# Modulation products in four column strips, and the first banded attention in batches of four heads

## The reference

```python
qb = q.reshape(B, nb, WINDOW, SWA_KV_HEADS, SWA_GROUP, HEAD_DIM)
kb, vb = band(k), band(v)               # the block before and the block itself
s = jnp.einsum('bnqhgd,bnkhd->bnhgqk', qb, kb) * (HEAD_DIM ** -0.5) + bias
s = jnp.where(mask, s, NEG_INF)
p = jax.nn.softmax(jnp.concatenate([s, sink], axis=-1), axis=-1)[..., :-1]
o = jnp.einsum('bnhgqk,bnkhd->bnqhgd', p, vb)
```

```python
mod = jax.nn.silu(c) @ w_ada + b_ada        # c: one row of 1024
mod_c = jax.nn.silu(c_ctx) @ w_ada + b_ada
```

## Time and profile before

| | |
|---|---|
| median of 3 runs | 2503.81 us (2503.61 to 2506.11) |
| span of the profiled execution | 2500.4 us |
| PE busy | 2411.0 us (96%) |
| DVE busy | 1599.2 us (64%) |
| ACT busy | 1248.2 us (50%) |
| POOL busy | 751.4 us (30%) |
| modulation and bias turn on PE | 54.38 to 85.95 us |
| banded attention on PE | 269.51 to 358.31 us |

### The profile page before, as it was taken

One profiled execution on the slowest core, in us unless ns is written; L12 is line 12 of the kernel. 1 busy time (PEld: TensorE's weight loads), 2 busy tenths in 40 slices (PEclk: granted clock), 3 DMA queues, 4 the chain that ended last, 5 costly groups with the idle time before them and its releaser, 6 DMA issues.

```text
span 2500.4 us, 32413 instructions
## 1 busy us (share of the span) xinstructions
PE 2411.0 (96%) x11302; PEld 1886.2 (75%) x11302; DVE 1599.2 (64%) x2478; ACT 1248.2 (50%) x1874; POOL 751.4 (30%) x396
## 2 busy tenths in 40 slices
PE   8999899999999999999999999999997999999996
PEld 6587567778788878878788778766764878878885
DVE  4033887756563357675442734687247999999998
ACT  4111555434543432443333411377245888888887
POOL 0312100114444477334466331120311132123310
PEclk9999999999999999999999999999998999999998
DMA  6210000022222264222233211000438999999996
GB/s 241 98 49 3 35 1 1 1 101 87 91 93 101 95 241 151 84 85 91 93 118 112 73 61 40 34 1 1 153 141 309 402 395 388 380 391 385 392 390 234
DMA packets 86602, 384.08 MB, mean 154 GB/s; under 512 B 7980, under 2 KB 9180, under 8 KB 71520
## 3 DMA queue, kind: packets, MB, share of 16 engines
q1 hardware_dynamic: 81744, 365.25, 38.7%
q0 software_dynamic: 4752, 17.43, 2.6%
HBM read 361.60 MB, written 21.05 MB: 153 GB/s over the span
## 4 chain that ended last, share of the span: by engine, by line
PE 49%; issue 11%; DVE 7%; POOL 4%; ACT 2%; DMA 1%; SPq 0%; POOLq 0%; DVEq 0%; ACTq 0%
PE ps L997 10%; PE ps L999 9%; PE ps L998 9%; PE ps L1367 5%; PE ps L1369 5%; PE ps L1368 5%; POOL w_lo L2816 4%; DVE e_lo L2672 3%; PE ps L1202 2%; PE ps L1192 1%; DMA arena<-in_w_gate 1%; PE ps L1274 1%; PE ps L1403 1%; DMA residual_rows<-arena 0%; PE ps L1181 0%
## 5 line engine op out<-in xcount | busy, mean ns | idle before, releaser
L2816 POOL TENSOR_TENSOR w_lo<-arena,w_hi 128x1024 fp32r<-128x1024 f32 x188 | 457.5, 2434 | 702.4 <-ACT w_hi L1608 700.1
L2672 DVE TENSOR_TENSOR e_lo<-arena,e_hi 128x1024 fp32r<-128x1024 f32 x384 | 451.3, 1219 | 35.4 <-ACT e_hi L1940 30.6
L1940 ACT ACTIVATE e_hi<-arena 128x1024 fp32r<-128x1024 f32 x384 | 401.3, 1059 | 88.1 <-PE ps L1369 82.0
L1608 ACT ACTIVATE w_hi<-arena 128x1024 fp32r<-128x1024 f32 x188 | 198.4, 1055 | 367.0 <-PE ps L999 366.9
L997 PE MATMUL ps<-h_hi,w_hi 128*128 128x512 f32 x848 | 336.4, 397 | 8.4 <-POOL w_lo L2816 5.3
L999 PE MATMUL ps<-h_hi,w_lo 128*128 128x512 f32 x848 | 332.0, 391 | 0.0
L998 PE MATMUL ps<-h_lo,w_hi 128*128 128x512 f32 x848 | 331.7, 391 | 0.0
L1367 PE MATMUL ps<-e_hi,x_hi 128*128 128x512 f32 x512 | 205.0, 400 | 7.2 <-DVE e_lo L2672 4.4
L1369 PE MATMUL ps<-e_lo,x_hi 128*128 128x512 f32 x512 | 200.2, 391 | 0.0
L1368 PE MATMUL ps<-e_hi,x_lo 128*128 128x512 f32 x512 | 200.0, 391 | 0.0
L997 PEld LDWEIGHTS ps<-h_hi,w_hi 128*128 128x128 f32 x848 | 160.4, 189 | 48.5 <-issue 12.2
(11 more groups left out here) (388 smaller groups left out, 5091.2 us busy)
## 6 DMA issues: line engine op xcount, KB each, us to landing
arena<-in_w_up SPq DMA_DIRECT2D x108, 1024.0 KB, 8.0
arena<-in_w_down SPq DMA_DIRECT2D x86, 1024.0 KB, 7.7
arena<-in_w_gate SPq DMA_DIRECT2D x64, 1024.0 KB, 10.0
arena<-in_w_in SPq DMA_DIRECT2D x18, 1024.0 KB, 4.8
arena<-in_w_out SPq DMA_DIRECT2D x16, 1024.0 KB, 4.8
arena<-in_w_ada SPq DMA_DIRECT2D x12, 1024.0 KB, 13.7
arena<-in_w_ada SPq DMA_DIRECT2D x24, 512.0 KB, 6.7
routed_rows<-arena SPq DMA_DIRECT2D x8, 520.0 KB, 7.5
```

The costliest lines, as they stand in the source:

```text
L1608: act_e.activation(w_hi[:, q, :], slot[c][:, q * D:(q + 1) * D], ACT.Copy).then_inc(s_whi, 1)
L1940: act_e.activation(e_hi[:, (2 * sl + a) % RING, :], slot[sl][:, a * D:(a + 1) * D], ACT.Copy).then_inc(s_ehi, 1)
L2672: v.tensor_tensor(e_lo[:, r, :], slot[sl][:, a * D:(a + 1) * D], e_hi[:, r, :].bitcast(F32), ALU.subtract).then_inc(s_elo, 1)
L2816: gp.tensor_tensor(w_lo[:, q, :], slot[c][:, q * D:(q + 1) * D], w_hi[:, q, :].bitcast(F32), ALU.subtract).then_inc(s_wlo, 1)
```

## The change

The modulation weights are used in two quads, (0, 1, 3, 4) and (7, 2, 6, 5). In a quad the product of each k goes to its own 32 partitions of the output (`ps[32 * j:32 * j + 32, ...]`), with a stationary operand of 32 columns, of which two are meant; so the four partial sums stand in four strips of the same bank. rowA takes all 128 rows, and `columns` multiplies with a constant ("pick") that adds the strips. The weights' buffers and the order of their loads change; item 0 of w_in is loaded before the last weights; ACT splits its two tiles as soon as the first quad is used; POOL's second constant waits for the end of the modulation, and w_out's loads wait for the end of the banded attention.

The banded attention goes by 16 quads of four heads (b; block n = b // 2). DVE still takes the maxima head by head. The sink stands as one more column before the scores (sw_raw has 257), so one exponential takes both and their sum. The transposes of a quad fill banks 4 (near block) and 5 (far block), which ACT and DVE copy with 512 columns each; eight value products follow, then one reciprocal of four columns and one product of 256 columns. The loops are written out.

```diff
-        rowA = view(156, 2 * D)[0:2]
+        rowA = view(156, 2 * D)
...
-            for k in range(4):
+            def modulation_weights(k):
                 sp.dma_start(adaA[k], ada[k, :, 0:2 * D]).then_inc(s_al[k], 16)
+            for k in (0, 1, 3, 4):
+                modulation_weights(k)
             sp.wait_ge(s_bld, 16)
             sp.wait_ge(s_h, 2)
             sp.wait_ge(s_sq, 2)
             sp.dma_start(mflip, bass.AP(ext_d, 0, [[1, P], [384, 8], [1, 256]])).then_inc(s_bias, 16)
-            for k in (4, 7):
-                sp.dma_start(adaA[k], ada[k, :, 0:2 * D]).then_inc(s_al[k], 16)
-            sp.wait_ge(s_au, 1)
-            sp.dma_start(adaA[5], ada[5, :, 0:2 * D]).then_inc(s_al[5], 16)
+            modulation_weights(7)
+            sp.wait_ge(s_h, 4)
+            sp.wait_ge(s_sq, 4)
+            modulation_weights(2)
+            sp.dma_start(slot[0], T["w_in"][:, 0:ITEM]).then_inc(wl[0], 16)
             sp.wait_ge(s_bc, 1)
-            sp.dma_start(adaA[6], ada[6, :, 0:2 * D]).then_inc(s_al[6], 16)
-
-
-            for i in range(7):
-                if i < 2:
-                    sp.wait_ge(s_au, 5)
+            modulation_weights(6)
+            sp.wait_ge(tps, 2 * T_IN)
+            modulation_weights(5)
+            for i in range(1, 7):
+                if i == 1:
...
+            sp.wait_ge(s_pv, U_DENSE)
...
-            def modulation(k, w, load, b, n):
-
-                pe.wait_ge(*load)
-                for c in range(n):
-                    m = pe.matmul(ps[0:2, b + c, :], scT[:, k, :], w[:, c * 512:(c + 1) * 512], start=(k == 0), stop=(k == KT - 1))
-                return m
-
             def columns(row, n, rows):
                 pe.wait_ge(s_row, rows)
                 for t in range(n):
-                    m = pe.transpose(ps[:, 4, 2 * t:2 * t + 2], row[:, t * P:(t + 1) * P], ident[0:2, 0:2])
+                    m = pe.matmul(ps[:, 4, 2 * t:2 * t + 2], row[:, t * P:(t + 1) * P], con("pick"), start=True, stop=True)
                 m.then_inc(s_mod, 1)
-            def modulations(ks):
-
-                for i in ks:
-                    k = ADA_ORDER[i]
-                    modulation(k, adaA[k], (s_al[k], 16), 4, 4).then_inc(s_au if k < KT - 1 else s_ad, 1)
+            def modulations(quad):
+                for k in ADA_QUADS[quad]:
+                    pe.wait_ge(s_al[k], 16)
+                for c in range(4):
+                    for j, k in enumerate(ADA_QUADS[quad]):
+                        m = pe.matmul(ps[32 * j:32 * j + 32, 4 + c, :], sc_wide[:, 2 * k:2 * k + 32], adaA[k][:, c * 512:(c + 1) * 512], start=(quad == 0), stop=(quad == 1))
+                m.then_inc(s_ad if quad else s_au, 1)
...
-            modulations(range(2))
+            modulations(0)
             pe.wait_ge(s_bias, 16)
             bias_turned(range(2, 4))
-            modulations(range(2, 4))
             pe.wait_ge(evv, 4)
             pe.wait_ge(eva, 4)
             bias_turned(range(2)).then_inc(s_flip, 1)
-            modulations(range(4, KT))
+            modulations(1)
...
+            def swa_scores(b, cs):
+                n, g, w = b // 2, b % 2, sw_keys(b)
+                if cs[0] == 0:
+                    pe.wait_ge(s_stage, n + 1)
+                if b >= 2:
+                    pe.wait_ge(s_max, 4 * (b - 2) + cs[-1] + 1)
+                for c in cs:
+                    m = pe.matmul(sw_scores(b, c), qs[n % 2][:, 4 * g + c, :], swak[:, (n + 1) * P - w:(n + 1) * P], start=True, stop=True)
+                    if c % 2:
+                        m.then_inc(s_S, 2)
+            def swa_turned(b, cs):
+                if cs[0] == 0 and b:
+                    pe.wait_ge(s_pt, 4 * b)
+                for c in cs:
+                    pe.wait_ge(s_exp, 4 * b + c + 1)
+                    for j in range(sw_keys(b) // P):
+                        m = pe.transpose(ps[:, 4 + j, c * P:(c + 1) * P], sw_probs[b % 2][:, c, 1 + j * P:1 + (j + 1) * P], ident)
+                if cs[-1] == 3:
+                    m.then_inc(s_T, 4)
+            def swa_values(b):
+                n, g, nb = b // 2, b % 2, sw_keys(b) // P
+                pe.wait_ge(s_pt, 4 * b + 4)
+                if b >= 2:
+                    pe.wait_ge(s_o, 4 * (b - 1))
+                for c in range(4):
+                    for j in range(nb):
+                        m = pe.matmul(ps[:, 6 + b % 2, c * HD:(c + 1) * HD], sw_turned[b % 2][j][:, c * P:(c + 1) * P], swav[:, n + 1 - nb + j, g * HD:(g + 1) * HD],
+                                      start=(j == 0), stop=(j == nb - 1))
+                m.then_inc(s_pv, 4)
...
-            units(U_SWA, swa(0, 0))
-            units(8, swa(1, 1), swa(0, 0))
-            with pe.Fori(1, NT // 2) as m:
-                for b in range(2):
-                    units(m * 16 + 8 * b, swa(2 * m + b, b), swa(2 * m + (b - 1), 1 - b))
+            swa_scores(0, range(4))
+            swa_scores(1, range(4))
+            for b in range(2 * NT):
+                for cs in (range(2), range(2, 4)):
+                    swa_turned(b, cs)
+                    if b + 2 < 2 * NT:
+                        swa_scores(b + 2, cs)
+                if b < 2 * NT - 1:
+                    swa_values(b)
...
+            act_e.wait_ge(s_au, 1)
+            for n in range(2):
+                first_high(n)
             act_e.wait_ge(s_flip, 2)
             act_e.activation(swab.rearrange("p a b -> p (a b)"), banks(0, 2048), ACT.Copy).then_inc(s_n1, 1)
-            for n in range(2):
-                first_high(n)
...
+            def swa_exp(b, c):
+                i, w = 4 * (b % 2) + c, sw_keys(b) + 1
+                act_e.wait_ge(s_max, 4 * b + c + 1)
+                if b >= 2 and c == 0:
+                    act_e.wait_ge(s_T, 4 * (b - 1))
+                    act_e.wait_ge(s_o, 4 * (b - 1))
+                act_e.activation(sw_probs[b % 2][:, c, 0:w], sw_raw[b % 2][:, c, 0:w], ACT.Exp, bias=sw_nmax[:, i:i + 1], scale=-1.0,
+                                 accum_out=sw_den[:, i:i + 1]).then_inc(s_exp, 1)
+            def swa_near_out(b):
+                act_e.wait_ge(s_T, 4 * b + 4)
+                if b >= 2:
+                    act_e.wait_ge(s_pv, 4 * (b - 1))
+                act_e.activation(sw_turned[b % 2][0], ps[:, 4, :], ACT.Copy).then_inc(s_pt, 2 if b >= 2 else 4)
+            act_e.wait_ge(s_ssi, 2)
+            for b in range(2 * NT):
+                swa_exp(b, 0)
+                if b:
+                    swa_near_out(b - 1)
+                for c in range(1, 4):
+                    swa_exp(b, c)
+                if b % 2 and b > 1:
+                    group_square(0, b // 2 - 1, 8 * (b // 2))
+            swa_near_out(2 * NT - 1)
...
+            def swa_max(b, c):
+                i, h, w = 4 * (b % 2) + c, 4 * (b % 2) + c, sw_keys(b)
+                v.wait_ge(s_S, 4 * b + c // 2 * 2 + 2)
+                if b >= 2:
+                    v.wait_ge(s_exp, 4 * (b - 2) + c + 1)
+                v.tensor_tensor_reduce(sw_raw[b % 2][:, c, 1:1 + w], sw_scores(b, c), swab[:, h, 256 - w:256], -1.0, sinkB[:, 0, h:h + 1],
+                                       ALU.add, ALU.min, sw_nmax[:, i:i + 1]).then_inc(s_max, 1)
+            def swa_far_out(b):
+                v.wait_ge(s_T, 4 * b + 4)
+                if b >= 4:
+                    v.wait_ge(s_pv, 4 * (b - 1))
+                v.tensor_copy(sw_turned[b % 2][1], ps[:, 5, :]).then_inc(s_pt, 2)
+            def swa_out(b):
+                n, four = b // 2, slice(4 * (b % 2), 4 * (b % 2) + 4)
+                v.wait_ge(s_pv, 4 * b + 4)
+                vc_.link(v.reciprocal(sw_rec[:, four], sw_den[:, four]))
+                v.tensor_tensor(mixed[:, n, b % 2 * 256:b % 2 * 256 + 256].rearrange("p (a b) -> p a b", a=4), ps[:, 6 + b % 2, 0:256].rearrange("p (a b) -> p a b", a=4),
+                                sw_rec[:, four].unsqueeze(2).to_broadcast([P, 4, HD]), ALU.mult).then_inc(s_o, 4)
...
+            for c in range(4):
+                swa_max(0, c)
+            for b in range(2 * NT):
+                if b + 1 < 2 * NT:
+                    for c in range(2):
+                        swa_max(b + 1, c)
+                if b:
+                    swa_out(b - 1)
+                if b + 1 < 2 * NT:
+                    for c in range(2, 4):
+                        swa_max(b + 1, c)
+                if b >= 2:
+                    swa_far_out(b)
```

More of the change, by code:

```diff
@@ L50 @@
 _at = 0
-for _n, _w in (("ident", P), ("causal", P), ("left", P), ("mean", P), ("swap16", P), ("swap32", P), ("flip", P), ("slot", 1)):
+for _n, _w in (("ident", P), ("causal", P), ("left", P), ("mean", P), ("swap16", P), ("swap32", P), ("flip", P), ("slot", 1), ("pick", 2)):
     CONST[_n] = (_at, _w)
@@ L478, in pair_columns @@
             return ps[:, 7, :]
-        def value_bank(w, dense):
-            return 6 if dense else 6 + w % 2
         def score_bank(u):
@@ L983, in late_turned @@
                     i.then_inc(s_flip, 1)
```

(9 more changed lines are left out.)

94 lines of the change are left out of this document (32 added, 62 removed).

## The result

| | before | after |
|---|---|---|
| median | 2503.71 us (2499.09 to 2506.11, 4 runs) | 2468.78 us (2467.59 to 2470.87, 4 runs) |
| ratio of the times | | 0.9865, 95% interval 0.9851 to 0.9879 |
| span of the profiled execution | 2500.4 | 2469.1 |
| modulation starts on PE | 54.38 | 56.72 |
| from there to tile 0 | 31.57 | 10.78 |

The forecast was 2471.0; the kernel takes 2468.8, by the ratio 1.35% less than before. The spans of the two profiled executions differ by 31.3 us, where the forecast's sum was 32.8; the medians differ by 34.9, because the profiled execution after is the slowest of its four, and the one before was faster than its median. The ledger of the two spans is the difference of the table's rows: start +2.3, modulation -20.8, tile 0 to scores +6.6, attention -19.1, rest -0.3, in all -31.3.

A forecast was written before the change was run, and what follows sets the result against it. PE was taken to bound the modulation, and DVE, with PE close behind, the banded attention. Forecast: 2500.4 - 13.9 (strips) + 2.6 (sums) - 21.5 (batches) = 2467.6, plus 3.4 around the span, 2471.0 us; range 2461 to 2487.

The forecast's parts named there:

- The strips: Modulation on PE: products in four strips half overlap, eight groups taking 13.9 us instead of 27.8, gain 13.9.
- Rival 1: Modulation: the four strips overlap fully, another 6.9 us off, 2464.1 us in all; chance 0.27.
- half overlap: Modulation: program order lets strip 1 start only beside strip 0's second record; 1.74 us a group, chance 0.42.
- full overlap: Modulation: all four strips run together, a group costing what one product does; gain 20.8 us, chance 0.27.
- The sums: PE, adding the strips: 32 matmul records replace 16 transposes, 3.7 us against 1.14, cost 2.6.
- Tile 0: First projection tile: split weights and bias copy ready 5 us ahead, or 1.6 with full overlap; no cost.
- The batches: Banded attention in quads of four heads: PE becomes the bound, gain 21.5 us; bounds 25 and 12.5.
- The cycle: Banded attention, steady part: one quad takes 4.5 us, bounds 4.2 and 5.2, for 13 cycles.
- The fill: Banded attention, first scores until the transposes of quad 2: about 6.8 us.
- Rival 3: Banded attention: copy before the value products exposed each time, 0.7 us a quad, 10 lost, 2481 us; chance 0.14.
- Rival 2: Modulation: strips do not overlap and gain nothing, summing costs 2.6, 2484.9 us in all; chance 0.13.
- Rival 4: Banded attention: TensorE's clock falls, some 65 us more if throughout, 2503 to 2537 us in all; chance 0.04.

The follow-up runs named there:

- one_strip: Kernel after, with all modulation products sent to strip 0 and the sums reading only those 32 rows: 2497.52 us, one run.
- strip_by_strip: Kernel after, with a quad's two loops exchanged so that four products of one strip stand in a row: 2475.81 us, one run.
- both_edits: Kernel after, with sums four at a time behind tiles 0 to 3 and each attention quad's scores after all its transposes: 2465.07 us, ratio 0.9850.
- sums_apart: Kernel after, with all 16 sums moved one tile ahead of the mean, behind tile 3: 2466.25 us, one run.
- transposes_thrice: Kernel before, with its sixteen 2-row transposes done three times over: 2507.1 us, one run.
- both_again: both_edits run once more, on one chip with the unaltered kernel after: 2465.24 us, ratio 0.9841.
- scores_last: Kernel after, with all transposes of an attention quad first and then all its scores: 2469.66 us, ratio 0.9874.
- strips_only: Kernel before, with only the strips, their sums and the moved loads: 2487.44 us, ratio 0.9936.
- batch_only: Kernel before, with only the batched attention and w_out's loads behind it: 2490.55 us, ratio 0.9940.
- sums_spread: Kernel after, with the 16 sums placed four each behind projection tiles 1 to 4: 2467.21 us, ratio 0.9857.

## Why the prediction was right, step by step

- **The strips** (gain 13.9 forecast, 20.8 measured): the step that failed is the supposition that PE starts its records in program order and that a second record of strip 0 holds back strip 1. Rival 1 held, to a tenth of a us: 8 groups take 7.2 us without the bias turn. one_strip and strip_by_strip show it: the records wait for their own strip, and a few that wait are passed. I had given half overlap 0.42 and full overlap 0.27. The two records of a product were a correct reading; what I drew from them about the start was not in any row.
- **The sums** (+2.6 forecast, +2.4 measured, 3.49 against 1.08): right, 0.109 a record against 0.115. (The row quoted for the 0.115, 1.95 us for 16, gives 0.122; the sum would have been 2.8.)
- **Tile 0** waits for nothing: right, and by the times of the full-overlap case: high parts until 62.4, low parts until 66.3, second quad done at 67.5. The cover forecast at 1.6 us is 1.2.
- **The batches** (gain 21.5 forecast, 19.1 measured; dense scores 69.7 us behind the first banded ones, 66.3 forecast). The cycle was right in its kind and nearly in size: 4.56 on the mean (267.22 to 326.44 in 13 cycles) against 4.5, PE the bound, DVE idle, the copy exposed by 0.13 where 0.05 was forecast. In it the transposes were over-counted (0.89 for 1.1) and the values under-counted: 1.84 for 1.55, 16 records at 0.115. The 0.39 of the earlier trace rows was the distance to the scores behind a unit's four value records; in a row of sixteen PEld is busy throughout (1.86), one load every 0.11 us, and the first load waits for the copy. The fill was 9.6 for 6.8: transposes of quad 2 stand behind the scores of quads 2 and 3, two times 1.75 us of PE, which the sum left out. With 2.8 us against 0.7 for the 13 cycles it is the larger miss of the two. Timeline of PE, the fill:

```profile
257.64 1.95 PE L938 MATMUL ps<-arena 128*128 128x128 f32 x16
260.57 0.71 PE L949 MATMUL ps<-const,arena 128*128 128x128 f32 x2 [0.98 <-ACT arena L1626]
261.12 1.04 PE L938 MATMUL ps<-arena 128*128 128x256 f32 x4
...
267.22 0.61 PE L949 MATMUL ps<-const,arena 128*128 128x128 f32 x4
```

- **Rival 3** (copy exposed by 0.7 a quad) did not come: 0.13. **Rival 2** did not: 3.6 a quad, not 14.
- **Rival 4** (the clock falls in the attention, and the kernel is slower) did not come: 1.00 from 258 to 326. (Short falls in that stage came in other executions, as in both_edits, and cost 1.7 us there.) But its mechanism came at a place where I had not looked, behind the sums, and smaller: the mean +1.6, shown by sums_apart, transposes_thrice and both_again to hang on how long the row of short records ahead of it is. With the slower tiles around 130 and falls between 225 and 255, tile 0 to the scores grew by 6.6, of which the sums are 2.4. Falls between 220 and 255 stand in eight of the ten executions with the new modulation stage or one_strip's form of it, at changing places (both_again: 0.66 at 245 to 250), but not in scores_last and strip_by_strip, and in none of the three with the old one. I have no cause for them.
- **The start** (+2.3, not forecast). The granted clock was 0.68 in the value products, at 20 to 25, where before it was 1.00:

```profile
20.00:25.00 5.00, 5.00 (x22) 5.00 (x21) 5.00 (x5) 5.00 (x6) 0.00 (x0) 0.68 1.01 423
```

 This start is there in both runs of the kernel after, in strips_only, one_strip, strip_by_strip, scores_last and both_again, and not in the kernel before, batch_only and transposes_thrice; but also not in sums_spread, sums_apart and both_edits, of which the last is the same program as both_again. So it is not tied to the program alone. Nor does the wait for n_lo just ahead of these products explain it: it is 1.57 us in the kernel before and 2.04 to 2.09 in all twelve others, with the fall or without. Of the kernels with the new modulation stage the three without the fall start it at 54.9 to 55.1 and the seven with it at 56.4 to 56.9; so some 1.7 of the 2.3 are the clock, and what tips it stays open.

That the total came so near was luck. In the sum an underrated gain of 6.9 met three costs that were not foreseen: 2.4 in the attention, some 4.2 of clock and tiles between tile 0 and the scores, 2.3 at the start. So the span fell 1.5 us less than the 32.8 forecast. The median came out 2.2 under the forecast all the same, for two reasons. The execution profiled after was 2.1 slower than its median. And the 3.4 us "around the span" mixed two things: 1.8 lies outside the span (2470.87 against 2469.1), and the other 1.6 was the distance of one execution from the median of several. The range, 2461 to 2487, had its lower end from full overlap, so it held what happened and not only the number.

## What to carry to other kernels

Products with few output rows gained nearly fourfold here when four of them went to four column strips, with neighbours in the program in different strips: the order (3.6, 8.9 or 13.9 us a quad here) is as much of the gain as the strips are. When a latency-bound loop is batched, count everything PE issues between the first score and the first steady cycle, and time a row of short matmuls by the pace of such a row (0.11 us a record here, with PEld busy throughout), not by the distance to whatever followed one of them. Do not put short matmuls side by side with other short ones: spread them between full tiles, since the cost (1.6 us on the mean, and tiles behind it) falls on instructions that nobody changed.

## What the runs showed of the hardware

- Two-record float32 products in four column strips overlap fully in alternating order: 32 records of 512 columns take 3.58 us from start to start, where one strip takes 13.85, a factor of 3.9. Four products in a row to the same strip give 8.8.
- TensorE's granted clock fell to its lower level while the profile had PE busy without a gap: behind 3 to 3.5 us of records with 2 columns or in the last of them, and through the records with one column (0.56 and 0.76 in two stretches of 5 us); with 1.1 us of them ahead it came later and shallower (0.70), or not at all. The Trainium skill, in "TensorE: Matmul & The Clock Gate", Part 1: The HAM clock gate, speaks of gaps between matmuls as what lets the clock fall; these rows show a fall with none between the records that the profile draws, whose ends are modelled.
- Executions of one kernel differ, and loosely with the mean granted clock: the kernel before gave spans of 2497.0 at 0.991 and 2505.4 at 0.985, but also 2501.1 and 2506.8 at 0.987. The two traces of one program, both_edits and both_again, have their short falls at different places. So one execution's span is no measure of an edit of 2 us, and the timeline of the stretch is the better one.
